# Products from tile 3 on, a head mix two tiles ahead, a new order of GpSimd's and SP's work in the MLP, and GpSimd's combinations in half pieces

## The reference

```python
h = rmsnorm(x, norm_mix)
proj = h @ w_in                      # 1024 -> 2312: q, k, v of two head groups, forget logits
out_a = swa_sink_attention(...)      # 8 heads, sliding window, learned sinks
out_b = forgetting_attention(...)    # 8 heads, causal softmax with forget bias
x = x + concat(out_a, out_b) @ w_out
h = rmsnorm(x, norm_mlp)
u = relu(h @ w_up)                   # 1024 -> 4096
x = x + (u * u) @ w_down
return rmsnorm(x, norm_final)
```

## Time and profile before

| what | value |
|---|---|
| runs | 2395.7, 2396.8, 2396.91 us; median 2396.8 |
| the profiled execution's own time | 2394.05 us |
| its span | 2392.4 us |
| PE busy | 2326.6 us (97%) |
| DVE busy | 1520.1 us (64%) |
| ACT busy | 1154.1 us (48%) |
| POOL busy | 706.9 us (30%) |
| DMA | 469.09 MB, mean 196 GB/s |
| mean granted TensorE clock | 0.995 |

### The profile page before, as it was taken

The page is one execution under the profiler, slowest core; times in us unless marked ns, Lnnn a source line. Parts: engine busy times, 40 slices in busy tenths (PEclk is TensorE's granted clock), DMA queues, the critical chain, the costliest instruction groups (busy, mean ns, idle before and its releaser), DMA issues.

```text
span 2392.4 us, 34959 instructions
## 1 busy us (share of the span) xinstructions
PE 2326.6 (97%) x11346; PEld 1934.7 (81%) x11346; DVE 1520.1 (64%) x2623; ACT 1154.1 (48%) x2226; POOL 706.9 (30%) x593
## 2 busy tenths in 40 slices
PE   7999999999999998999899999999999999999998
PEld 5888888788888886887687877888888888888887
DVE  6588873688888886566745655444465555564454
ACT  5211112788888886223545555555553233333243
POOL 2000000111111114235568764666640032120132
PEclk9999999999999999999999999999999999999999
DMA  5567765666666565766455576654457486564464
GB/s 189 215 235 278 268 242 163 180 160 156 160 157 157 152 156 169 248 218 202 170 183 163 189 286 242 202 160 152 154 190 260 165 298 234 193 219 162 138 219 160
DMA packets 253970, 469.09 MB, mean 196 GB/s; under 512 B 59336, under 2 KB 119752, under 8 KB 246032
## 3 DMA queue, kind: packets, MB, share of 16 engines
q1 hardware_dynamic: 247808, 451.11, 58.6%
q0 software_dynamic: 6048, 16.52, 2.6%
HBM read 316.13 MB, written 151.42 MB: 195 GB/s over the span
## 4 chain that ended last, share of the span: by engine, by line
PE 51%; DVE 3%; POOL 2%; issue 2%; DMA 1%; ACT 1%; SPq 0%; POOLq 0%; ACTq 0%; DVEq 0%
PE m_ps L2533 24%; PE m_ps L2556 23%; PE m_ps L1685 4%; DMA b_kept<-f_kept 1%; POOL m_mix L1548 1%; DVE f_up_lo L2389 1%; PE m_ps L2574 0%; DVE m_xn L1653 0%; DVE m_xm L1646 0%; DVE m_mix L1622 0%; ACT m_mix_hi L1585 0%; DVE keep_lo L2408 0%; POOL h_raw L1560 0%; POOL f_kept L2157 0%; DVE hop_lo L1659 0%
## 5 line engine op out<-in xcount | busy, mean ns | idle before, releaser
L2556 PE MATMUL m_ps<-keep_hi,hop_hi 128*128 128x512 f32 x880 | 342.5, 389 | 0.4 <-DVE hop_lo L2392 0.4
L2556 PE MATMUL m_ps<-keep_hi,hop_lo 128*128 128x512 f32 x880 | 342.4, 389 | 0.0
L2556 PE MATMUL m_ps<-keep_lo,hop_hi 128*128 128x512 f32 x880 | 342.3, 389 | 0.0
L2392 DVE TENSOR_TENSOR hop_lo<-h_raw,hop_hi 128x512 fp32r<-128x512 f32 x224 | 176.6, 789 | 236.8 <-ACT hop_hi L2228 236.7
L2389 DVE TENSOR_TENSOR f_up_lo<-wide_raw,f_up_hi 128x512 fp32r<-128x512 f32 x160 | 182.5, 1142 | 223.0 <-ACT f_up_hi L2223 222.9
L2228 ACT ACTIVATE hop_hi<-h_raw 128x512 fp32r<-128x512 f32 x224 | 140.8, 630 | 334.4 <-PE m_ps L2556 330.5
L958 POOL DMA_DIRECT2D o_main<-a_o x63 | 36.5, 580 | 775.2 <-ACT a_o L1326 726.6
L599 PE MATMUL p_ps_o<-p_ht_lo,p_w_hi 128*128 128x512 f32 x576 | 224.5, 390 | 0.0
L2533 PE MATMUL m_ps<-keep_hi,f_up_hi 128*128 128x512 f32 x512 | 202.8, 396 | 6.1 <-DVE f_up_lo L2389 4.7
L2533 PE MATMUL m_ps<-keep_hi,f_up_lo 128*128 128x512 f32 x512 | 201.3, 393 | 0.0
L2533 PE MATMUL m_ps<-keep_lo,f_up_hi 128*128 128x512 f32 x512 | 199.4, 390 | 0.0
(11 more groups left out here) (246 smaller groups left out, 5779.8 us busy)
## 6 DMA issues: line engine op xcount, KB each, us to landing
h_raw<-u_ops SPq DMA_DIRECT2D x224, 256.0 KB, 4.2
wide_raw<-in_w_up SPq DMA_DIRECT2D x32, 1024.0 KB, 7.2
u_ops<-f_u SPq DMA_DIRECT2D x128, 256.0 KB, 4.3
wide_raw<-in_x SPq DMA_DIRECT2D x59, 512.0 KB, 4.0
u_ops<-f_us SPq DMA_DIRECT2D x96, 256.0 KB, 2.3
proj_hi<-p_o_hi SPq DMA_DIRECT2D x17, 1024.0 KB, 6.2
proj_lo<-p_o_lo SPq DMA_DIRECT2D x17, 1024.0 KB, 8.3
h_raw<-in_w_down SPq DMA_DIRECT2D x58, 256.0 KB, 3.9
```

The costliest lines, as they stand in the source:

```text
L2392: nc.vector.tensor_tensor(lo, a_raw[:, (m - UP) % A_RING], hi.bitcast(F32), ALU.subtract).then_inc(op_lo_done, 1)
L2556: last = nc.tensor.matmul(down_banks[b % 2][t][:], a[:, cols], w[j], start=(j == 0 and m == 0), stop=(j == FG - 1 and m == 2))
```

## The change

The change touches five places; none of the arithmetic changes.

- Start: `product_after_turn` becomes 3, 5, 8, 10, 12, 14 for products 0 to 5, and `GATE_TILE` 5. Products 6 and 7 follow turn 15. Squares of the first tiles run two tiles ahead and write to another scratch tile; the splits of w_in for the two column pairs stand after tile 2 and tile 3, one each, and product 0 waits for the first alone; VectorE's norm of tile 4 stands behind the second.
- Head mix: `join`, `divide` and `split_mix` prepare tile t + 2 in step t, not t + 1. On ScalarE `split_mix(t + 2)` stands behind `square(t)` and ahead of `copy_ht(t - 1)`; on VectorE `divide(t + 2)` stands between the additions and the norm, the split behind the norm. The order of SP's DMAs stays.
- GpSimd's combinations: `combine` makes each of 512 columns as two of 256; `mix_tokens` of the MLP (4 x 512) becomes 8 instructions, `mix_rest` and the mix stage's `mix_tokens` (2 x 512) 4 and 2.
- Order in the MLP: `mix_w(g + 1, 3)` moves ahead of `mix_rest`, and for g = 15 ahead of `mix_u(14)`, which there waits for hop (1, 2), not hop (1, 1). `LAST_TILE` is 3.
- SP: at g = 15 `load_parts(4)` stands ahead of `store_rest(14)`, `load_parts(5)` and `(6)` behind it, and `load_w(17)` last. `store_token_mix` stands ahead of `load_w`.

```diff
-        squares = whole.raw["p_o_hi0"][:, S - D:S]
+        squares = whole.raw["keep_hi"][:].rearrange("p (k b) s -> p k (b s)", k=DK // 2)[:, :, S - 2 * P:S]
...
-        GATE_TILE = 7
+        GATE_TILE = 5
...
-        product_after_turn = {t: 2 * (t // TPB - 1) + t % TPB // 2 for t in range(TPB, ST) if t % 2}
+        product_after_turn = {t: n for n, t in enumerate((3, 5, 8, 10, 12, 14))}
...
             square(0)
+            square(1)
             for t in range(ST):
-                if t + 1 < ST:
-                    square(t + 1)
+                for ahead in range(t + 1, min(t + 3, ST)):
+                    if ahead == (t + 2 if ahead < X_RING else t + 1):
+                        square(ahead)
                 if t in product_before_turn:
                     split_first(product_before_turn[t])
                 split_ht_hi(t)
-                if t == 2:
-                    split_w_hi(0)
-                    split_w_hi(1)
+                if t in (2, 3):
+                    split_w_hi(t - 2)
...
-                if t + 1 < ST:
+                if t + 1 < ST and t != 3:
                     norm(t + 1)
...
-                if t == 2:
-                    split_w_lo(0)
-                    split_w_lo(1)
+                if t in (2, 3):
+                    split_w_lo(t - 2)
+                if t == 3:
+                    norm(t + 1)
...
-                pe.wait_ge(w_lo_done, 2)
+                pe.wait_ge(w_lo_done, min(n, 1) + 1)
...
+            join(1)
             for t in range(ST):
-                if t + 1 < ST:
-                    join(t + 1)
+                if t + 2 < ST:
+                    join(t + 2)
...
+            split_mix(1)
             for t in range(ST):
-                if t + 1 < ST:
-                    split_mix(t + 1)
-                else:
+                if t == ST - 1:
                     mlp.scalar_first(act)
                 act.wait_ge(added, HALVES * (t + 1))
...
                                      accum_out=ssum[:, t:t + 1]).then_inc(squared, 1)
+                if t + 2 < ST:
+                    split_mix(t + 2)
                 if t:
                     copy_ht(t - 1)
...
+                if t + 2 < ST:
+                    divide(t + 2)
                 if t == ST - 1:
                     mlp.vector_second(dve)
...
                                                ALU.mult, ALU.mult).then_inc(normed, 1)
+                if t + 2 < ST:
+                    split_mix(t + 2)
...
-    LAST_TILE = 2
+    LAST_TILE = 3
...
         for g in range(GROUPS):
+            if g == FG - 1:
+                load_parts(4)
             if g:
                 store_rest(g - 1)
+            if g in rest_stored_at:
+                store_token_mix(rest_stored_at[g])
+            if g == FG - 1:
+                load_parts(5)
+                load_parts(6)
             if g + 2 < GROUPS:
                 load_w(g + 2)
...
-            if g in rest_stored_at:
-                store_token_mix(rest_stored_at[g])
...
-            if g == FG - 1:
-                for i in sorted(PRE_ORDER):
-                    load_parts(i)
...
+    def combine(dst, a, b, op):
+
+        half = dst.shape[1] // 2
+        for cols in (slice(0, half), slice(half, 2 * half)):
+            last = nc.gpsimd.tensor_tensor(dst[:, cols], a[:, cols], b[:, cols], op)
+        return last
...
-                nc.gpsimd.tensor_tensor(s1[:], a21, a22, ALU.add).then_inc(w_mixed, 1)
+                combine(s1[:], a21, a22, ALU.add).then_inc(w_mixed, 1)
...
             if g == FG - 1:
-                pool.wait_ge(hop_lo_done, hop_count[1, 1])
+                mix_w(g + 1, 3)
+                pool.wait_ge(hop_lo_done, hop_count[1, 2])
             if g:
                 mix_u(g - 1)
+            if g + 1 < GROUPS and g != FG - 1:
+                mix_w(g + 1, 3)
             if 2 <= g < 10:
                 mix_rest(*divmod(g - 2, 2))
-            if g + 1 < GROUPS:
-                mix_w(g + 1, 3)
```

More of the change, by code:

```diff
@@ L445, in _ @@
                 split_ht_hi(t)
-                if t == 2:
-                    split_w_hi(0)
-                    split_w_hi(1)
-            for n in range(2 * SB - 3, 2 * SB - 1):
+                if t in (2, 3):
+                    split_w_hi(t - 2)
+            for n in range(2 * SB - 2, 2 * SB - 1):
                 split_first(n)
@@ L1559, in mix_tokens @@
                     pool.wait_ge(hop_lo_done, 2)
-                nc.gpsimd.tensor_tensor(dst[:, k], a[:, k], b[:, k], ALU.subtract).then_inc(t_mixed, 1)
+                for m in range(k.start, k.stop):
+                    last = nc.gpsimd.tensor_tensor(dst[:, m], a[:, m], b[:, m], ALU.subtract)
+                last.then_inc(t_mixed, 1)
             pool.sem_inc(joined, 1)
             pool.wait_ge(mhalf_set, 1)
+            join(1)
             for t in range(ST):
-                if t + 1 < ST:
-                    join(t + 1)
+                if t + 2 < ST:
+                    join(t + 2)
                 if t == ST - 1:
@@ L2123, in mix_u @@
                 pool.wait_ge(us_out[2], 16 * g)
-            nc.gpsimd.tensor_tensor(us[2][:], u21[b][:], us[1][:], ALU.subtract).then_inc(u_mixed, 1)
+            combine(us[2][:], u21[b][:], us[1][:], ALU.subtract).then_inc(u_mixed, 1)
         def mix_tokens():
             pool.wait_ge(hop_lo_done, hop_count[0, 3])
-            nc.gpsimd.tensor_tensor(raw[:, 2], raw[:, 2], raw[:, 0], ALU.subtract).then_inc(t_mixed, 1)
+            for k in range(4):
+                last = combine(raw[:, 2, k], raw[:, 2, k], raw[:, 0, k], ALU.subtract)
+            last.then_inc(t_mixed, 1)
         def mix_rest(n, half):
@@ L2142, in mix_rest @@
                 dst, a, b = raw[:, 0], raw[:, 1], raw[:, 0]
-            nc.gpsimd.tensor_tensor(dst[:, k], a[:, k], b[:, k], ALU.subtract).then_inc(t_mixed, 1)
+            for m in range(k.start, k.stop):
+                last = combine(dst[:, m], a[:, m], b[:, m], ALU.subtract)
+            last.then_inc(t_mixed, 1)
         def mix_b(i, j):
```

27 lines of the change are left out of this document (13 added, 14 removed).

## The result

The changed kernel took 2412.8 us (median of 4 runs, 2411.55 to 2413.53), the kernel before 2396.86 in the same set (4 runs); the ratio is 1.0067, 95% interval 1.0052 to 1.0082. That is slower by 15.9 us, 0.67%. Forecast were 2405.5 and a slower kernel. The profiled execution of the changed kernel took 2413.53 us.

A forecast was written before the change was run, and what follows sets the result against it. TensorE, busy 97% of the span, was taken to bound the kernel, so only its idle time and clock count. Terms summed to +9.0 us on the 2396.8 median, 2405.8, taken as 2405.5; range 2392 to 2413.

The forecast's parts named there:

- the forecast's own case: Whole kernel: the time comes out as the terms sum, 2401 to 2410 us; chance 0.4.
- Start, +5.4: Start: product 0 begins 6.5 us earlier, but later waits and half clock cost more; +5.4 us, bounds +3 and +7.
- Head mix, +0.9: Head mix, tiles 9 to 15: late joins and splits go (-5.7 us), new loop waits come; +0.9, bounds -5.7 and +4.
- the landing in the loop: Head mix: from copy's end to landed inverses 9.0 us, some 0.4 overlapping, in a loop of 14.3 us a tile.
- Half pieces, 0: GpSimd's combinations: 0.2 us more per 512 columns, nearly nothing on the path; 0, bounds -1 and +1 us.
- First up products, +0.5: First up products: waits for C1's copy (2.9 us) and before up 6 (3.9), half clock after; +0.5, bounds -2.5 and +2.
- Waits inside the up phase, -2.5: Up phase: the wait at 1258 goes, that at 1380 shrinks to 0.3; -2.5 us, bounds -3 and -1.
- Switch, +4.7: Switch at g 15: late mix_u(14) and w queued last make waits 8.2 us against 4.7; +4.7, bounds -4.7 and +7.
- the faster one (the DMA loops don't bind): Head mix and switch: loads land early enough that neither new DMA loop binds; 2390 to 2392.5 us, chance 0.13.
- Rival 3: GpSimd's port: VectorE gets in between any two pieces, taking 4 us from the sum; 2401.5 us, chance 0.12.
- Rival 4: Clock: each new wait is followed by 3 us at half clock, none of the old spared; 2410 to 2412, chance 0.15.

## Why the prediction was right, and where it was off

The direction held, and most of the mechanisms; the sizes did not. The time came out 7.3 us above the forecast, 0.2 us inside the upper end of the range (2413) and outside the 2401 to 2410 of the forecast's own case: that the range holds it is partly luck. Between the profiles the program lost 19.5 us where the sum has 9.0, and most of the difference lies in two terms, the head mix (4.7) and the switch (3.5).

1. *Start, +5.4.* Right. Distance at 99 us: +4.1 in the changed kernel, +3.0 to +7.1 in the seven others with that start; the start alone costs 0.16%. The scatter goes with the clock: full speed came back between 23.7 and 26.4 us, and in the four runs of 6.0 to 7.1 it fell once more behind product 6's wait, near 77.
2. *Head mix, +0.9.* Right in mechanism, wrong in size: +5.6. The failed step is the landing in the loop. It was set at 9.0 less 0.4 and took 10.4 us. Of these 1.8 us, 1.1 are a misreading: the 9.0 ends with the first of the two DMAs that bring the inverses, and the second landed 10.1 us after the store's issue in the kernel before too. The overlap of 0.4 didn't come. With the hand-overs the loop is 16.1 us a tile, not 14.3, so the waits are 7.1 us and not 4.3 to 5.5. The clock fell once, as allowed, but it stood at half from 1120.2 to 1127.1, and from turn 12 to turn 13 it took 16.1 us, 3.1 more than 11.87 and the wait of 1.12 in it, where the term allowed 1.7. Undoing the one swap on ScalarE won 11.3 us of stage time.
3. *Half pieces, 0.* The bounds of -1 to +1 were wrong. Alone they cost 0.39%, 9 us. I priced a piece by its time alone, 0.2 us more per 512 columns, and let the port help VectorE only. The runs showed the other side. At the switch of the kernel with half pieces alone each of the eight pieces of 256 columns in mix_u(14) took 0.74 to 1.73 us while VectorE's subtractions ran, against 0.72 alone, and so a pair took 1.9 to 3.4 us where a whole one took 1.6 to 2.2 in the kernel before; mix_u is a chain that SP's stores and loads wait for. That each piece waits anew for VectorE is read from these durations; the traces don't show the port. In the changed kernel mix_u(14) stands behind hop (1, 2), and only one of its four pairs is so long (3.29 us). At the switch the pieces alone cost 4.1 us, the orders alone 6.3 (the run with whole pieces) and both together 8.2: they overlap, so the 8.2 can't be shared out between them. Undoing one left the other in force (5.1 stayed with hop (1, 1), 4.2 to 7.4 with the old orders). With whole pieces and SP's better order together the switch is 1.6 to 2.5 us shorter than in the kernel before.
4. *First up products, +0.5.* +1.9. The waits merged as drawn: 2.64 for the copy (2.9 forecast) and one of 4.35 before up 6 (3.9). Behind the second the clock stood at half for 6.8 us, where the forecast priced one fall (1.3). The nine kernels with half pieces lie at +0.2 to +1.9 here, the three with whole pieces and the mix two tiles ahead at -0.8 to -1.1, so the pieces set the sign. LAST_TILE is worth nothing either way (-1.0 us with 3 and with 2, both with whole pieces).
5. *Waits inside the up phase, -2.5.* -2.0: the one at 1258 went whole; the one at 1380 fell from 1.24 to 0.90, not to 0.3, and half pieces are not what sets it: in the nine kernels that have them it is 0.47 to 1.95, in the four without 1.11 to 1.24.
6. *Switch, +4.7.* +8.2. The order of events was right (up 114's wait 2.38, w_up last, one long wait). The program was 10.4 us behind by then; less that, w_up landed at 1487.6 and not 1485, and up 118 started at 1489.7 and not 1487.2. 1.3 of these 2.5 us were there at the issue of part 5 (1480.71 - 10.4 = 1470.3, against 1469), the rest in the queue: the first part landed 6.2 us after its issue, as the term has it (3.7 and 2.5, though no row shows the 3.7), each further one 2.4 to 2.5 later, but w_up 3.65 behind the last of them and not 2.5. The other 1 us is clock: 2.7 us more were lost behind up 118 than in the kernel before, and 1.7 forecast.

Of the rivals, the faster one (the DMA loops don't bind) fell: both loops bound. Rival 3, VectorE let in at each seam, is true of VectorE: its busy time was 24 us shorter in the changed kernel than with whole pieces (1449.5 and 1473.6 us), and 54 us shorter with half pieces alone than in the kernel before (1466.0 and 1520.1). It was of no use to the end. Rival 4, the clock, given a chance of 0.15, has the time nearest to the one measured (2410 to 2412), and its falls came: the clock stood at half at each of the new waits that it names (near 42, 1121, 1158, 1175 and 1496 us). From turn 9 to the end of the switch it stood there for 27 us, against 7 in the kernel before, each stretch 3.4 to 10.2 us long where 3 were assumed. But the waits too were longer than summed (7.1 us against 4.3 to 5.5 in the head mix, 11.7 against 8.2 at the switch), and of that the rival says nothing.
